# Three instead of two tile pairs of each gate/up block by seven products, with the turned tiles in the last banks, and another order at the begin of the feed-forward

## The reference, cut to what matters

```python
h = h + rmsnorm(merged @ w_out[i], post_mix_g[i])
u = rmsnorm(h, pre_ffn_g[i])
ff = (jax.nn.silu(u @ w_gate[i]) * (u @ w_up[i])) @ w_down[i]
h = h + rmsnorm(ff, post_ffn_g[i])
```

## Time and profile before

| | |
|---|---|
| median of 3 runs | 1088.6 us (1088.55 to 1089.33) |
| the profiled execution | 1089.17 us, span 1086.7 us, mean granted clock 0.998 |
| TensorE busy | 1074.7 us (99%), 5795 matmuls |
| VectorE busy | 832.6 us (77%) |
| ScalarE busy | 575.0 us (53%) |
| DMA | 208 MB, mean 191 GB/s |

### The profile page before, as it was taken

The page is one execution under the profiler, slowest core; times in us unless marked ns, Lnnn a source line. Parts: engine busy times, 40 slices in busy tenths (PEclk is TensorE's granted clock), DMA queues, the critical chain, the costliest instruction groups (busy, mean ns, idle before and its releaser), DMA issues. The chain is left out here.

```text
span 1086.7 us, 15213 instructions
## 1 busy us (share of the span) xinstructions
PE 1074.7 (99%) x5795; PEld 931.1 (86%) x5795; DVE 832.6 (77%) x1047; ACT 575.0 (53%) x703; POOL 27.4 (3%) x46
## 2 busy tenths in 40 slices
PE   9999999999999999999999999999999999999997
PEld 8999999999888888888888888888888888888885
DVE  5699886637646776787887977877878888777787
ACT  6554454736554565554554554544545555554553
POOL 4000001101000000000000000000000000000000
PEclk9999999999999999999999999999999999999999
DMA  8655535444386385665656656656556666656664
GB/s 270 213 175 168 163 117 155 137 136 136 120 308 211 117 284 181 213 191 180 216 189 195 211 167 201 209 179 213 192 195 202 224 199 207 195 187 222 198 202 179
DMA packets 113206, 208.05 MB, mean 191 GB/s; under 512 B 9184, under 2 KB 46496, under 8 KB 111856
## 3 DMA queue, kind: packets, MB, share of 16 engines
q1 hardware_dynamic: 111952, 201.49, 57.9%
q10 hardware_dynamic: 608, 4.20, 0.9%
q0 software_dynamic: 576, 1.40, 0.4%
HBM read 202.86 MB, written 4.19 MB: 191 GB/s over the span
## 5 line engine op out<-in xcount | busy, mean ns | idle before, releaser
L550 ACT ACTIVATE w_hi<-raw 128x1024 fp32r<-128x1024 f32 x336 | 352.3, 1059 | 296.1 <-PE ps L1703 206.0
L903 DVE TENSOR_TENSOR w_lo<-raw,w_hi 128x1024 fp32r<-128x1024 f32 x336 | 406.6, 1226 | 131.1 <-ACT w_hi L550 130.5
L1701 PE MATMUL ps<-w_hi,uf 128*128 128x512 f32 x584 | 228.6, 392 | 0.9 <-DVE w_lo L903 0.6
L1703 PE MATMUL ps<-w_hi,uf 128*128 128x512 f32 x584 | 227.4, 389 | 0.0
L1702 PE MATMUL ps<-w_lo,uf 128*128 128x512 f32 x584 | 227.2, 389 | 0.0
L1365 PE MATMUL ps<-u,w_hi 128*128 128x272 f32 (+1 forms) x544 | 158.8, 292 | 0.0
L1367 PE MATMUL ps<-u,w_hi 128*128 128x272 f32 (+1 forms) x544 | 155.9, 287 | 0.0
L1368 PE MATMUL ps<-u,w_lo 128*128 128x272 f32 (+1 forms) x544 | 155.7, 286 | 0.0
L1701 PEld LDWEIGHTS ps<-w_hi,uf 128*128 128x128 f32 x584 | 109.6, 188 | 23.4 <-DVE w_lo L903 0.8
L1703 PEld LDWEIGHTS ps<-w_hi,uf 128*128 128x128 f32 x584 | 109.6, 188 | 23.0
L1702 PEld LDWEIGHTS ps<-w_lo,uf 128*128 128x128 f32 x584 | 109.7, 188 | 22.4
(11 more groups left out here) (273 smaller groups left out, 1301.1 us busy)
## 6 DMA issues: line engine op xcount, KB each, us to landing
raw<-in_w_gate SPq DMA_DIRECT2D x176, 256.0 KB, 3.0
raw<-in_w_up SPq DMA_DIRECT2D x176, 256.0 KB, 3.4
raw<-in_w_down SPq DMA_DIRECT2D x88, 512.0 KB, 4.1
raw<-in_w_in SPq DMA_DIRECT2D x72, 512.0 KB, 3.8
raw<-in_w_out SPq DMA_DIRECT2D x32, 512.0 KB, 4.2
arena<-in_x SPq DMA_DIRECT2D x2, 1024.0 KB, 6.4
arena<-in_x ACTq DMA_DIRECT2D x2, 1024.0 KB, 8.3
out<-h2rows SPq DMA_DIRECT2D x2, 1024.0 KB, 5.5
```

The source lines that it names most:

```text
L550: act.activation(w_hi[:, slot, :], raw[:, slot, :], ACT.Copy).then_inc(hi_done, 1)
L903: dve.tensor_tensor(w_lo[:, slot, :], raw[:, slot, :], hi_view(w_hi[:, slot, :]), ALU.subtract).then_inc(lo_done, 1)
L1701: pe.matmul(o, a[0], b[0], start=start, stop=False)
L1703: return pe.matmul(o, a[1], b[0], start=False, stop=stop)
```

## The change

- `SEVEN_F` gets a third pair, and `ROUND` of blocks 1 to 10 becomes PPZPZPZP instead of PPPZPZPP: three pairs of seven products, the last one directly before the last plain pair. `FOLD` follows from it (chunk 13 instead of 11). Three sets of row sums are made in block 0, at chunks 10, 12 and 14.
- `inner` goes: the inner product is written over `gated`. `silu` then waits for the turn before (`f_turned`).
- The turn stands ahead of chunk 2 instead of 3 and goes to the last two banks of the half. The order of the sevens' banks becomes m1, m5, m7, m6. The copies of the turned tiles stand at chunk 5 (`INNER_AT`) instead of 6. A block's first Z waits for `f_lo` ahead of m7, not ahead of m1.
- At the begin of the feed-forward, the second chunk is split ahead of the first input tiles on ScalarE and on VectorE, and the idle matmuls are 3 and 9 instead of 8, 6 and 6.
- Two taps go from chunk 45 to chunk 47.

```diff
--- before.py
+++ after.py
@@ -89,7 +89,7 @@
     TAP_ORDER = [(w, t) for pair in range(CT // 2) for w in range(TAPS) for t in (2 * pair, 2 * pair + 1)]
     TAPS_AT, n_taps = {}, 0
     for q in range(TAP_FROM, SC + PER_G + 4):
-        many = 0 if q in (POOL_AT, POOL_AT + 1) else 1 if q - NEAR in PAIR_AT else 2 if q + 1 - SUMS - NEAR in PAIR_AT else 4
+        many = 0 if q in (POOL_AT, POOL_AT + 1, pair_at(2) + SUMS + NEAR - 1) else 1 if q - NEAR in PAIR_AT else 2 if q + 1 - SUMS - NEAR in PAIR_AT else 4
...
@@ -124,11 +124,11 @@
...
-    SEVEN_F, SEVEN_U = (0, 1), (13, 14, 15, 16, 17, 18, 19)
+    SEVEN_F, SEVEN_U = (0, 1, 2), (13, 14, 15, 16, 17, 18, 19)
     SUM_AT = {4: 13, 11: 14, 13: 15, 19: 16, 21: 17, 27: 18, 29: 19}
     SUM_NO = {d: i for i, d in enumerate(SUM_AT.values())}
-    F_SUM_AT = {12: 0, 14: 1}
-    ROUND = ["PPPPPPPP"] + ["PPPZPZPP"] * (NFG - 1) + ["PPPPZPPPZPPPZPPPZPPZPP", "PPPZPPZPPZPPZPPZPZPZPP"]
+    F_SUM_AT = {10: 0, 12: 1, 14: 2}
+    ROUND = ["PPPPPPPP"] + ["PPZPZPZP"] * (NFG - 1) + ["PPPPZPPPZPPPZPPPZPPZPP", "PPPZPPZPPZPPZPPZPZPZPP"]
...
 
@@ -143,6 +143,7 @@
     SEVENS_TO = [sum(1 for k, _ in SEVENS if k <= g) for g in range(NG)]
     FOLD = [2 * ROUND[g].rindex("Z") + 1 if "Z" in ROUND[g] else -1 for g in range(NG)]
...
+    INNER_AT = 5
     FOLDS_F = len(QUARTERS) * (NFG - 1)
...
 
@@ -195,10 +196,9 @@
         a_y = place(4 * KT * SEQ)
...
         sums_f = sb_at("sums_f", [P, len(SEVEN_F), 4, 2, P], F32R, a_y)
-        gated = sb_at("gated", [P, NQ, DCOLS], F32, a_y + 4 * KT * SEQ - 16 * DCOLS)
-        inner = sb_at("inner", [P, NQ, DCOLS], F32, a_y + 4 * KT * SEQ - 8 * DCOLS)
+        gated = sb_at("gated", [P, NQ, DCOLS], F32, a_y + 4 * KT * SEQ - 8 * DCOLS)
         sums_y = sb_at("sums_y", [P, max(len(SEVEN_U) - IN_U, 1), 3, 2, P], F32R, a_y)
...
         cst = sb_at("cst", [P, 1152], F32, a_c)
@@ -779,8 +779,8 @@
...
             split(Q_FFN)
+            split(Q_FFN + 1)
             first_input_hi(0, 0, 1)
-            split(Q_FFN + 1)
             first_input_hi(0, 2, 3)
...
@@ -807,13 +807,13 @@
...
-                    act.wait_ge(p_done, NQ * b)
+                    act.wait_ge(f_turned, b)
                     act.activation(gated[:, m, :], quarter(b, m, 0), ACT.Silu, scale=r2c[:, m:m + 1]).then_inc(silu_done, 1)
 
             def inner_hi(b):
                 act.wait_ge(f_turned, b + 1)
                 act.copy(ffn[:, 4 * b:4 * b + 4, 0, :],
-                         ps[:, 4 * (b % 2):4 * (b % 2) + 2, :].rearrange("p b (c t) -> p (b c) t", c=2)).then_inc(f_hi, 1)
+                         ps[:, 4 * (b % 2) + 2:4 * (b % 2) + 4, :].rearrange("p b (c t) -> p (b c) t", c=2)).then_inc(f_hi, 1)
 
...
@@ -867,7 +867,7 @@
...
                     if 1 <= g <= NFG and ch == 3:
                         silu(g - 1)
-                    if 1 <= g <= NFG and ch == 6:
+                    if 1 <= g <= NFG and ch == INNER_AT:
                         inner_hi(g - 1)
                     if g == 0 and ch - 1 in F_SUM_AT:
                         input_sums_hi(F_SUM_AT[ch - 1])
@@ -1162,13 +1162,13 @@
                     if b:
                         dve.wait_ge(fold_done, len(QUARTERS) * (b - 1) + NQ + m + 1)
                         dve.wait_ge(f_turned, b)
-                    dve.scalar_tensor_tensor(inner[:, m, :], quarter(b, m, 1), r2c[:, m:m + 1], gated[:, m, :],
+                    dve.scalar_tensor_tensor(gated[:, m, :], quarter(b, m, 1), r2c[:, m:m + 1], gated[:, m, :],
                                              ALU.mult, ALU.mult).then_inc(p_done, 1)
 
             def inner_lo(b):
                 dve.wait_ge(f_hi, b + 1)
                 dve.tensor_tensor(ffn[:, 4 * b:4 * b + 4, 1, :],
-                                  ps[:, 4 * (b % 2):4 * (b % 2) + 2, :].rearrange("p b (c t) -> p (b c) t", c=2),
+                                  ps[:, 4 * (b % 2) + 2:4 * (b % 2) + 4, :].rearrange("p b (c t) -> p (b c) t", c=2),
                                   hi_view(ffn[:, 4 * b:4 * b + 4, 0, :]), ALU.subtract).then_inc(f_lo, 1)
 
...
@@ -1255,7 +1255,7 @@
 
             def fold_sums(g):
 
-                m1, m6, m5, m7 = (sevens_bank(g, k) for k in range(4))
+                m1, m5, m7, m6 = (sevens_bank(g, k) for k in range(4))
...
@@ -1740,8 +1740,6 @@
                     pe.wait_ge(s_lo, 2 * (SEVEN_F.index(d) + 1))
                 else:
                     pe.wait_ge(s_lo, 2 * (SUM_NO[d] + len(SEVEN_F) + 1))
-                if begin and g <= NFG:
-                    pe.wait_ge(f_lo, g)
                 if begin and g > NFG:
                     pe.wait_ge(f_done, len(QUARTERS))
                 three(m1, left(g, 2 * d, 0), right(q, 0), begin, end).then_inc(chunks_used, 1)
@@ -1750,6 +1748,8 @@
                 three(quarter(g, 0, 1), row_sum(2), right(q + 1, 1)).then_inc(chunks_used, 1)
                 pe.wait_ge(t_lo_done, 2 * z + 1)
                 three(m5, row_sum(0), weight_sum(0), begin, end).then_inc(t_used, 1)
+                if begin and g <= NFG:
+                    pe.wait_ge(f_lo, g)
                 three(m7, row_sum(3) if g < NFG else left(g, 2 * d, 1), weight_sum(1), begin, end).then_inc(t_used, 1)
                 pe.wait_ge(t_lo_done, 2 * z + 2)
                 three(m6, row_sum(1), weight_sum(2), begin, end).then_inc(t_used, 1)
@@ -1761,7 +1761,7 @@
                 for m in range(NQ):
                     for t in range(4):
                         at = t % 2 * SEQ + m * P
-                        mm = pe.transpose(ps[:, 4 * (b % 2) + t // 2, at:at + P], inner[:, m, t * P:(t + 1) * P], ident)
+                        mm = pe.transpose(ps[:, 4 * (b % 2) + 2 + t // 2, at:at + P], gated[:, m, t * P:(t + 1) * P], ident)
                 mm.then_inc(f_turned, 1)
 
...
@@ -1772,12 +1772,10 @@
             pe.wait_ge(y_done, NQ * DN_OUT - 1)
             for ch in range(2):
                 plain_products(Q_FFN + ch, [(0, 0), (0, 1)])
-                if ch == 0:
-                    idle(8)
-            idle(6)
+            idle(3)
             pe.wait_ge(rows_done, 2)
             turn(0, [1])
-            idle(6)
+            idle(9)
             pe.wait_ge(y_done, NQ * DN_OUT)
             for ch in range(2):
                 plain_products(Q_FFN + ch, [(1, 0), (1, 1)]).then_inc(chunks_used, 1)
@@ -1796,7 +1794,7 @@
                 chs = 2 * len(ROUND[g])
                 for ch in range(chs if g < NG - 1 else chs - LAST):
                     q = BEGIN[g] + ch
-                    if g <= NFG and ch == 3:
+                    if g <= NFG and ch == 2:
                         turn_inner(g - 1)
                     if (g, TURNS[g][ch // 2]) not in SEVEN_NO:
                         plain_products(q, QUARTERS).then_inc(chunks_used, 1)
```

More of the change, by code:

```diff
@@ L197, in build_trunk @@
         sums_f = sb_at("sums_f", [P, len(SEVEN_F), 4, 2, P], F32R, a_y)
-        gated = sb_at("gated", [P, NQ, DCOLS], F32, a_y + 4 * KT * SEQ - 16 * DCOLS)
-        inner = sb_at("inner", [P, NQ, DCOLS], F32, a_y + 4 * KT * SEQ - 8 * DCOLS)
+        gated = sb_at("gated", [P, NQ, DCOLS], F32, a_y + 4 * KT * SEQ - 8 * DCOLS)
         sums_y = sb_at("sums_y", [P, max(len(SEVEN_U) - IN_U, 1), 3, 2, P], F32R, a_y)
-        assert 32 * P * len(SEVEN_F) + 16 * DCOLS <= 4 * KT * SEQ and 24 * P * (len(SEVEN_U) - IN_U) <= 4 * KT * SEQ
+        assert 32 * P * len(SEVEN_F) + 8 * DCOLS <= 4 * KT * SEQ and 24 * P * (len(SEVEN_U) - IN_U) <= 4 * KT * SEQ
         side = sb_at("side", [P, KT * SEQ], F32, a_y)
```

## The result

Median of 4 runs each, side by side: 1088.76 us before (1088.55 to 1089.33), 1078.55 us after (1078.32 to 1078.69). The ratio is 0.9905 (0.9892 to 0.9917): 10.2 us faster. On the 1088.6 us of the table that is 1078.3 us. The forecast was 1079.3, a gain of 9.3; its range ended at 1078.5. The sign and the mechanism came as forecast, the size 1 us larger.

What follows compares the result with a forecast made beforehand. TensorE's instruction list plus three short waits was taken as the bound. Third seven pair 6.80, begin 1.75 and taps 0.75 sum to 9.3 us, so 1088.6 becomes 1079.3 us, range 1078.5 to 1083.5.

Steps and rivals of the forecast that it cites:

- What bounds: Whole kernel: the time is the number of instructions TensorE issues, plus three short waits of 0.72, 0.60 and 0.26 us.
- 1. Third seven pair: Blocks 1 to 10: three products fewer each, 30 x 0.2268 = 6.80 us less on TensorE, blocks of 42.39 us.
- 2. The walk: One new block, engine by engine in queue order: VectorE and ScalarE deliver in time, cost 0, slacks 0.6 to 1.75 us.
- 3. Row sums: Block 0: a third set, about 2.5 us of VectorE between splits due much later, cost 0.
- 4. The begin: Start of the feed-forward: second chunk's split pulled ahead, earlier turn and restart, gain 1.75 us (0.86 to 2.0).
- 5. The taps: Ahead of the value products: two taps moved from chunk 45 to 47, gain 0.75 us (0.6 to 0.8).
- The sum: Whole kernel: 6.80 + 1.75 + 0.75 = 9.3 us, taken alike from span, profiled time and median, giving 1079.3 us.
- A: Blocks: one slack (turn, m7 or block start) is used up in each, 4 us, 1083.3; chance 13%.
- B: Begin of the feed-forward: gives only its idle pieces or less, 0 to 0.9 instead of 1.75 us, 1080.6; chance 8%.
- C: Begin of the feed-forward: fewer idle products let TensorE's clock fall to 1.2 GHz, 5.4 us, 1084.7; chance 2%.
- D: Blocks: VectorE becomes the bound; with two thirds of its idleness staying, 1101 us, slower; chance 4%.
- E: Outside the sevens, as the last block's handover to the down projection: takes back 6 to 9 us, no change; chance 2%.

Runs made afterwards that it cites:

- after again: The changed kernel, unchanged, timed and profiled once more: 1078.95 us, ratio 0.9907 to the kernel before.
- the additions: Changed kernel with four two-input 128x512 additions more on VectorE behind the inner product in each of blocks 1 to 10: 1091.21 us.
- the copies: Changed kernel with four 128x512 copies more on VectorE behind the inner product in each of blocks 1 to 10: 1080.86 us.

## Why the prediction was right or wrong

**What bounds: right.** TensorE's list and its three short waits. After: no idle piece, 42.40 of 42.40 us busy, and TensorE's last product starts 9.3 us earlier, counted from the first input turn (1056.23 against 1065.55).

**1. Third seven pair, 6.80 us: right.** Blocks of 42.39 us, and 6.7 to 6.8 us between the kernels with two and with three. The Trainium skill ("TensorE: Matmul & The Clock Gate", Back-to-back issue gap) gives 216 and 131 ns for the pitch; the estimates from them, 6.5 and 3.9 us, both miss the measured term. The pitch of 0.227 us from the trace holds. VectorE 38.8 us a block, 39.1 forecast.

**2. The walk, cost 0: right, to within 0.05 us at four places.** VectorE's timeline of after, block 5, which begins at 586.63 - 5.44 = 581.19:

```profile
581.48 2.49 DVE L1273 TENSOR_TENSOR ps<-ps,tx 128x512 f32<-128x512 f32 x4 [0.44 <-PE ps L1703]
...
585.20 1.22 DVE L903 TENSOR_TENSOR w_lo<-raw,w_hi 128x1024 fp32r<-128x1024 f32 x1
...
592.94 1.22 DVE L1170 TENSOR_TENSOR ffn<-ps,ffn 128x1024 fp32r<-128x1024 f32 x1
...
619.04 0.69 DVE L1262 TENSOR_TENSOR tx<-ps,tx 128x512 f32<-128x512 f32 x1 [0.80 <-ACT tx L884]
```

Relative to the block's start: folds at 0.29 (walked 0.29), products done at 4.01 (4.01), inner_lo at 11.75 (11.76), fold sums 4.54 ahead of the next block (4.5). The splits of chunks 11 and 15 end 0.1 us later than walked. Of the slacks, that at m7 is shown by load: 1.46 us more just fit, 2.52 don't, by 1.05 with the 0.16 that the bracket leaves out, so it is 1.45 to 1.5. In block 1, 1.13 us more overshoot by 0.17 + 0.16 and 1.46 by 0.49 + 0.16: a slack of 0.8 by both, as walked. The price of not moving the wait, 1.2 us, was 1.46 a block: 1.16 to 1.19 of recorded idle time and 0.28 more that a stop costs, which the forecast had left out. The slacks at the turn and at the block's start were not tried alone; no stop shows at them.

**3. Row sums, cost 0: right.** From the begin's last turn to block 1's turn: 423.33 - 374.30 = 49.03 before, 417.07 - 370.75 = 46.32 after, plus a chunk of 2.72 for the earlier turn, 49.04.

**4. The begin, 1.75 us: right,** 1.77 in the profiles and 1.7 to 1.85 with it undone. Its intermediate times too, shifted by the 1.78 us that were gained ahead of it: the turn was forecast for 368.0 - 1.78 = 366.2 and stands at 366.26, the restart for 367.8 and stands at 367.84.

**5. The taps, 0.75 us: right,** 0.79 in the profiles and 0.7 to 0.8 undone.

**The sum: the step that failed.** The terms were right: 6.80 + 1.75 + 0.75 = 9.3, and 9.3 to 9.5 were gained between the first input turn and the end. What failed is the step from there to the time. The forecast took 9.3 from the span, from the profiled time and from the median alike, so it held everything else constant without a reason.

First, the "about 2.5 us" outside the span were carried over at a change of 0. They fell by 0.45 to 0.5 (2.44 to 1.93 in the mean), and this part belongs to the change. With it the forecast would have been 1078.8, inside the range. Second, the start-up was taken as equal. It scatters by 1.3 us from one execution to the next. In the profiled pair this adds 0.99 us. In the medians of four runs a side it leaves some tenths: the four runs of after have spans of 1076.4 to 1076.8, where those of after again go up to 1077.8. Over all executions with a span on record, 42 of before and 8 of after, the means are 10.3 us apart, 9.8 in the span and 0.5 outside. The 0.4 between these 9.8 and the 9.3 to 9.5 of the anchored spans are not told apart from chance by eight executions.

So it took both for the time to come out under the range's end of 1078.5: a term of 0.5 us that the forecast had at nothing, and about as much luck of the start-up. The range's low end, 0.8 us under the forecast, gave the working of the known terms room and nothing for these two.

**The rivals.** A (a slack used up in each block) fell: turns 42.39 us apart. B fell: 1.77 us. C fell: the granted clock was 1.00 in the begin's window, TensorE busy 8.00 of 8.00 us. D (VectorE becomes the bound) fell for this change. Its reasoning from a share of idleness that stays was the wrong model: with 94% of VectorE busy TensorE loses 0.14 us a block in one kernel and 1.2 in the other. E fell: the tail is the same.

## What to carry to other kernels

Where one engine issues without a break, a change is worth its instructions times their measured pitch, if the in-order walk of the other engines through one period closes; the walk, with the slack at each wait, was good to 0.1 us here, while the busy share of the second engine said nothing. Whether a slack is used up shows in the distance between equal places of two periods sooner than in idle pieces. The instruction that the bound engine waits for should stand as early as possible in its own engine's queue and the wait as late as possible in the other's: that placement alone was worth 15 us against a saving of 7. In comparing profiles, anchor them behind the start-up and take the time outside the span from several executions; one profiled pair can differ by a microsecond for no reason of the change.

## What the runs showed of the hardware

- A stop of TensorE costs 0.27 to 0.32 us beyond its recorded idle time (12.4 us idle, 15.2 us cost, ten stops; 0.9 idle, 1.2 cost a block with the additions). A product that comes hardly late (0.24 instead of 0.227 us) costs 0.14 us with no idle time recorded.
- A single-input fp32 copy of 128x512 on VectorE takes 0.35 us, a two-input addition 0.60. The Trainium skill, "VectorE: DVE Perf Modes", The perf-mode tier table, states that fp32 copies within SBUF run at twice the base rate and `tensor_tensor` at the base rate; the trace agrees in that the copy is the faster, by 1.7 times at 512 columns, which the expectation of the copies had left out.
- Time outside the span has two levels, 2.44 and 1.93 us in the mean (2.28 to 2.60 and 1.89 to 1.99), and 20 more instructions on VectorE (1067 for 1047) switch from the first to the second; 40 more on ScalarE don't.
- The start-up scatters by 1.3 us (first input turn at 11.64 to 12.97) in kernels that are the same up to there, one with fewer warm-up matmuls (11.90) aside. In it the idle 128x128 matmuls run at two rates, ten in 2.3 us or in 1.4, while the granted clock's column gives full speed throughout: in these first microseconds the column doesn't show the rate.
